# A first mixture of experts that adds its last four units by matrix multiplication instead of gathers

## The reference

```python
def moe_ffn(h, router_w, router_b, w_gate, w_up, w_down):
    ...
    w = jnp.take_along_axis(s, ids, axis=1)
    w = w / jnp.sum(w, axis=-1, keepdims=True)
    combine = jnp.sum(jax.nn.one_hot(ids, N_EXPERTS, dtype=jnp.float32) * w[..., None], axis=1)
    y = jnp.zeros(h.shape, jnp.float32)
    for e in range(N_EXPERTS):
        a = jax.nn.silu(h @ w_gate[e]) * (h @ w_up[e])
        y = y + combine[:, e:e + 1] * (a @ w_down[e]).astype(jnp.float32)
    return y.astype(h.dtype)
...
        x_lat = x_lat + g2 * ff_lat.reshape(x_lat.shape)
    return rms_norm(x_lat, final_g)
```

## Time and profile before

| | |
|---|---|
| median of 3 runs | 2612.09 us |
| profiled execution | 2609.95 us, span 2608.1 us |
| TensorE matmul busy | 2150.4 us (82%) |
| VectorE busy | 1245.8 us (48%) |
| ScalarE busy | 775.8 us (30%) |
| GpSimd busy | 203.5 us (8%) |
| DMA | 684.69 MB, mean 263 GB/s |

### The profile page before, as it was taken

How to read it: one execution, slowest core, us unless ns; L and a number is a source line. 1 busy time by engine, 2 the same in 40 slices (tenths; PEclk the granted TensorE clock), 3 DMA queues, 4 the chain that set the end, 5 groups by cost and what they waited for, 6 DMA issues and landing times. The chain is left out here.

```text
span 2608.1 us, 43444 instructions
## 1 busy us (share of the span) xinstructions
PE 2150.4 (82%) x18242; PEld 1499.7 (58%) x18242; DVE 1245.8 (48%) x1976; ACT 775.8 (30%) x1304; POOL 203.5 (8%) x202
## 2 busy tenths in 40 slices
PE   4999999896974999887778766899998887768765
PEld 3977777794542789543334335677777644334333
DVE  3367676645223544543333336666555653233334
ACT  4266666432113323211111114444423411111112
POOL 2010000101101000000000001111111000000001
PEclk8999999997997999898889887999999999889978
DMA  9157675438998233899999982211113699999995
GB/s 355 47 187 242 224 243 195 130 98 351 407 421 293 86 98 121 343 399 417 419 418 419 416 354 83 65 50 50 45 48 138 247 388 417 418 417 418 412 410 212
DMA packets 211850, 684.69 MB, mean 263 GB/s; under 512 B 23021, under 2 KB 122038, under 8 KB 152502
## 3 DMA queue, kind: packets, MB, share of 16 engines
q1 hardware_dynamic: 198742, 646.01, 64.4%
q0 software_dynamic: 8912, 21.04, 2.3%
q10 hardware_dynamic: 3984, 14.68, 1.4%
HBM read 671.68 MB, written 21.00 MB: 266 GB/s over the span
## 5 line engine op out<-in xcount | busy, mean ns | idle before, releaser
L221 PE MATMUL PS<-second 128*128 128x256 f32 (+1 forms) x4944 | 930.9, 346 | 54.2 <-DVE second L251 21.0
L221 PEld LDWEIGHTS PS<-second 128*128 128x128 f32 x4944 | 761.3, 193 | 200.3 <-DVE second L251 28.3
L221 PE MATMUL PS<-ring,arena 128*32 128x256 f32 (+5 forms) x6288 | 662.7, 453 | 208.9 <-DMA ring<-in_moe_w_down 65.6
L221 PEld LDWEIGHTS PS<-ring,arena 128*32 128x32 f32 (+2 forms) x6288 | 311.3, 124 | 449.6 <-issue 308.9
L221 PE MATMUL PS<-arena 128*32 128x256 f32 (+10 forms) x2480 | 496.1, 383 | 77.1 <-DMA ring<-in_moe_w_up 21.3
L221 PEld LDWEIGHTS PS<-arena 128*32 128x32 f32 (+4 forms) x2480 | 245.9, 151 | 241.2 <-issue 170.9
L233 ACT ACTIVATE arena<-PS 128x256 f32<-128x256 f32 (+2 forms) x218 | 106.5, 488 | 583.2 <-PE PS L221 506.0
L240 DVE TENSOR_TENSOR arena<-PS,arena 128x512 f32<-128x512 f32 (+1 forms) x305 | 210.5, 690 | 91.6 <-PE PS L221 64.7
L233 ACT ACTIVATE arena<-arena 128x128 f32<-128x128 f32 (+4 forms) x299 | 176.0, 589 | 191.8 <-DVE arena L240 67.3
L240 DVE TENSOR_TENSOR second<-ring,second 128x1024 fp32r<-128x1024 f32 (+1 forms) x90 | 149.0, 1656 | 156.1 <-ACT second L233 150.7
L240 DVE TENSOR_TENSOR arena<-arena,PS 128x256 f32<-128x256 f32 (+1 forms) x77 | 40.9, 531 | 372.3 <-PE PS L221 371.2
(11 more groups left out here) (170 smaller groups left out, 1358.3 us busy)
## 6 DMA issues: line engine op xcount, KB each, us to landing
ring<-in_moe_w_down SPq DMA_DIRECT2D x124, 1024.0 KB, 16.3
ring<-in_moe_w_up SPq DMA_DIRECT2D x121, 1024.0 KB, 15.4
ring<-in_moe_w_gate SPq DMA_DIRECT2D x109, 1024.0 KB, 16.6
ring<-in_ada_w SPq DMA_DIRECT2D x48, 1024.0 KB, 5.3
arena<-in_moe_w_gate SPq DMA_DIRECT2D x28, 1024.0 KB, 12.8
ring<-in_w_mod SPq DMA_DIRECT2D x22, 1024.0 KB, 7.0
arena<-in_moe_w_up SPq DMA_DIRECT2D x19, 1024.0 KB, 14.4
spare<-in_moe_w_gate SPq DMA_DIRECT2D x17, 1024.0 KB, 15.7
```

What stands on the lines that cost most here:

```text
L221: return P.e.matmul(o, l, r, start=st, stop=sp)
```

## The change

- Rows of units 8 to 11 no longer go to `y_d`. VectorE multiplies them with `GROW`, ScalarE and VectorE split the weighted rows into two fp32r parts (`down_ve`, `down_ac`), VectorE makes the 0/1 matrix (`where_late_ve`), and TensorE adds them to the tokens: unit 8 in iteration 10, unit 9 in iteration 11, units 10 and 11 together after the branch of the conditional units (`combine_late_pe`). VectorE adds the sums to `x` (`late_ve`).
- Two `shared` conditions fall, so the places and shares of these rows are computed early in the first mixture (`shares_pe`, `shares_ve`, `share_ve`, `columns_ve`).
- The eight gathers read only rows of units 0 to 7 and are issued once the gate matmuls of unit 11 are done. Their buffers move to the place of `XN` and `H2T` and are zero-filled by GpSimd, two in each of iterations 5 to 8.
- VectorE mixes tile 0 before it evicts unit 11 and tile 1 after it, both ahead of the branch. The order of the end is written out, and the last scaling to `XN` goes from ScalarE to VectorE.
- The router weights of the second mixture are loaded behind the second load of the convolution.

```diff
--- before.py
+++ after.py
@@ -1293,6 +1293,18 @@
+    LATE = 8
+    LATE_ROWS = [YP, *([second[AR0 + o][:, 2048 + 1024 * i:3072 + 1024 * i] for i in range(2)] for o in (12288, 27136))]
+    LATE_WT = [second[AR0 + 27136][:, 1024:1536], second[AR0 + 27136][:, 1536:2048], second[AR0 + 30976][:, 256:768]]
+    def late(n):
+        return (n + 1) % 2 if n < LATE + 4 else 2
+    def before_late(m, n):
+        return at("ps", "cm", m.i, n - 2 if n < LATE + 4 else n - 1, 3, 1) if n > LATE + 4 or LATE + 1 < n < LATE + 4 else None
@@ -1444,11 +1456,10 @@
-            else:
-                self.tokf, self.ws = tmp(NB, 4), tmp(NB)
+            self.tokf, self.ws = tmp(NB, 4), tmp(NB)
             self.tz, self.idx = tmp(NB), tmp(NB).bitcast(i32)
             self.ei, self.eii, self.nvi = tmp(NOV), tmp(NOV).bitcast(i32), tmp(1).bitcast(i32)
-            self.ybuf = [view(o + 1024 * j, F) for o, k in ((16384, 4), (14336, 2), (29768, 2)) for j in range(k)]
+            self.ybuf = [view(o + 1024 * t, F) for t in range(4) for o in (4096, 8192)]
@@ -1620,8 +1631,8 @@
-        if m.i < 2:
-            router_sp(MO[m.i + 1])
+        if m.i == 1:
+            router_sp(MO[2])
@@ -1688,6 +1699,37 @@
+    def late_pe(b, n, t, f, first, last):
+        W, rows_ = LATE_WT[late(n)], LATE_ROWS[late(n)]
+        for j in range(2):
+            i = mm(b, W[:, 128 * t:128 * t + 128], rows_[j][:, 512 * f:512 * f + 512], first and j == 0, last and j == 1)
+        return i
+    def combine_extra_pe(m, n):
+        P.wait_ge(at("W", m.i, n), at("ev", "down", m.i, n, 1))
+        for t in range(4):
+            for f in range(2):
+                late_pe(take(state["units"], "cm", m.i, n, t, f), n, t, f, True, True).then_inc(*P.mark("ps", "cm", m.i, n, t, f))
+    def combine_late_pe(m):
+        a, z = LATE + 2, LATE + 3
+        P.wait_ge(at("W", m.i, z), at("ev", "down", m.i, a, 1))
+        b4 = {}
+        for t in range(2):
+            for f in range(2):
+                b4[t, f] = take(state["units"], "cm", m.i, z, t, f)
+                late_pe(b4[t, f], a, t, f, True, False)
+        P.wait_ge(at("ev", "down", m.i, z, 1))
+        for t in range(4):
+            for f in range(2):
+                if t > 1:
+                    b4[t, f] = take(state["units"], "cm", m.i, z, t, f)
+                    late_pe(b4[t, f], a, t, f, True, False)
+                late_pe(b4[t, f], z, t, f, False, True).then_inc(*P.mark("ps", "cm", m.i, z, t, f))
@@ -1760,7 +1802,7 @@
-        b = take(state["units"], name, m.i, done=({"tok": "idx", "tok2": "idx2"}[name] if m.i == 0 else {"tok": "tokf", "tok2": "tokf2"}[name], m.i))
+        b = take(state["units"], name, m.i, done=("tokf2" if name == "tok2" else "tokf" if m.i else "idx", m.i))
@@ -1845,6 +1887,8 @@
+                if n > LATE + 1:
+                    combine_extra_pe(m, n - 2)
@@ -1855,8 +1899,7 @@
-                if m.shared:
-                    shares_pe(m, "share2", m.NV)
+                shares_pe(m, "share2", m.NV)
@@ -1871,10 +1914,14 @@
+            if m.shared is None:
+                combine_extra_pe(m, n)
...
+        else:
+            combine_late_pe(m)
@@ -1900,6 +1947,18 @@
+        if n >= LATE:
+            hi, lo = LATE_ROWS[late(n)]
+            V.wait_ge(at("ps", "frow", 1))
+            for f in range(2):
+                c = slice(512 * f, 512 * f + 512)
+                V.wait_ge(at("ps", "down" if f else "down0", m.i, n))
+                tt(DIAG[:, c], bank("down", m.i, n, f), GROW[:, c], ALU.mult, "gy", m.i, n, f)
+            for f in range(2):
+                c = slice(512 * f, 512 * f + 512)
+                V.wait_ge(at("hi", "y", m.i, n, f))
+                stt(lo[:, c], DIAG[:, c], m.ws[:, n:n + 1], hi[:, c].bitcast(f32), ALU.mult, ALU.subtract, "ev", "down", m.i, n, f)
+            return
@@ -1910,6 +1969,25 @@
+    def where_late_ve(m, n):
+        V.wait_ge(before_late(m, n))
+        tt(LATE_WT[late(n)].rearrange("p (t s) -> p t s", s=128), bc(iota[:, :].unsqueeze(1), 4, 128), bc(m.tokf[:, n, :].unsqueeze(2), 4, 128), ALU.is_equal, "W", m.i, n)
+    def late_ve(m, n, t):
+        for f in range(2):
+            o = x[:, t, 512 * f:512 * f + 512]
+            V.wait_ge(at("ps", "cm", m.i, n, t, f))
+            tt(o, bank("cm", m.i, n, t, f), o, ALU.add, "ev", "cm", m.i, n, t, f)
+    def mix_ve(m, t):
+        V.wait_ge(at("comb", m.i, 2 * t))
+        stt(m.ybuf[2 * t], m.ybuf[2 * t], m.w12[:, t, 0:1], x[:, t, :], ALU.mult, ALU.add)
+        V.wait_ge(at("comb", m.i, 2 * t + 1))
+        stt(x[:, t, :], m.ybuf[2 * t + 1], m.w12[:, t, 1:2], m.ybuf[2 * t], ALU.mult, ALU.add)
@@ -2124,20 +2202,17 @@
-                shares_ve(m, "share2", m.NV)
+            shares_ve(m, "share2", m.NV)
...
-                share_ve(m, "share2", m.NS, m.NB)
+            share_ve(m, "share2", m.NS, m.NB)
...
-                columns_ve(m, m.NS, m.NB)
+            columns_ve(m, m.NS, m.NB)
@@ -2159,6 +2234,8 @@
+            if m.shared is None and n in (LATE - 2, LATE - 1):
+                where_late_ve(m, n + 2)
@@ -2171,6 +2248,10 @@
+                if n > LATE + 1:
+                    for t in range(4):
+                        late_ve(m, n - 2, t)
+                    where_late_ve(m, n)
@@ -2183,7 +2264,11 @@
         count = count_of(m, V)
+        if m.shared is None:
+            mix_ve(m, 0)
         down_ve(m, m.NP - 1)
+        if m.shared is None:
+            mix_ve(m, 1)
 
@@ -2193,6 +2278,10 @@
+            if m.shared is None:
+                where_late_ve(m, n)
+                for t in range(4):
+                    late_ve(m, n, t)
@@ -2220,18 +2309,25 @@
-        def mix(t):
-            V.wait_ge(at("comb", m.i, 2 * t))
-            stt(XN[:, t, :], m.ybuf[2 * t], m.w12[:, t, 0:1], x[:, t, :], ALU.mult, ALU.add)
-            V.wait_ge(at("comb", m.i, 2 * t + 1))
-            stt(x[:, t, :], m.ybuf[2 * t + 1], m.w12[:, t, 1:2], XN[:, t, :], ALU.mult, ALU.add, "mix", m.i, t)
         def final(t):
             V.wait_ge(at("sq", "m0", t))
             stt(x[:, t, :], x[:, t, :], rs[:, t:t + 1], FROW, ALU.mult, ALU.mult, "x", "m0", t)
 
-        V.wait_ge(at("ev", ("row", m.i), 1), at("ev", "frow", 1))
-        tiles_ve(mix, final)
+        V.wait_ge(at("ev", "frow", 1))
+        late_ve(m, LATE + 3, 0)
+        late_ve(m, LATE + 3, 1)
+        final(0)
+        mix_ve(m, 2)
+        late_ve(m, LATE + 3, 2)
+        final(1)
+        mix_ve(m, 3)
+        late_ve(m, LATE + 3, 3)
+        norm_x_ve("m0", 0)
+        final(2)
+        norm_x_ve("m0", 1)
+        final(3)
+        norm_x_ve("m0", 2)
+        norm_x_ve("m0", 3)
@@ -2250,6 +2346,14 @@
+        if n >= LATE:
+            hi = LATE_ROWS[late(n)][0]
+            A.wait_ge(at("ev", "share2", m.i), *((at("y", m.i, LATE - 2), at("y", m.i, LATE - 1)) if n == LATE + 1 else ()), before_late(m, n))
+            for f in range(2):
+                c = slice(512 * f, 512 * f + 512)
+                A.wait_ge(at("gy", m.i, n, f))
+                act(hi[:, c], DIAG[:, c], ACT.Copy, "hi", "y", m.i, n, f, scale=m.ws[:, n:n + 1])
@@ -2315,15 +2419,19 @@
-        overflow(m, A, count, one, D("y0"), D("y1"))
+        overflow(m, A, count, one)
...
-            A.wait_ge(at("ev", "cm", m.i, m.NB - 1, t, 1) if m.shared else at("mix", m.i, t))
+            A.wait_ge(at("ev", "cm", m.i, m.NB - 1 if m.shared else LATE + 3, t, 1))
...
-            tiles_ac(name, first, lambda t: again_ac(name, t))
+            first(0)
+            for t in range(4):
+                if t < 3:
+                    first(t + 1)
+                again_ac(name, t)
@@ -2357,6 +2465,16 @@
+            if 5 <= n <= 8 and m.i == 0:
+                G.wait_ge(at("xn_d", m.i), at("ps", "down", m.i, 0), at("ps", "gu", m.i, 2, 0))
+                for o in m.ybuf[2 * n - 10:2 * n - 8]:
+                    fill(o, 0.0, "yz")
+        if m.shared is None:
+            G.wait_ge(at("yi", m.i), at("y", m.i, LATE - 2), at("y", m.i, LATE - 1), at("yz"), at("ps", "gu", m.i, LATE + 3, 0))
+            for i in range(8):
+                G.e.indirect_dma_start(
+                    out=m.ybuf[i], out_offset=None, in_=m.y_d, in_offset=bass.IndirectOffsetOnAxis(ap=m.yi[:, i // 2, i % 2:i % 2 + 1], axis=0),
+                    bounds_check=LATE * m.R - 1, oob_is_err=False).then_inc(*state["comb"][i].next("comb", m.i, i))
         count = count_of(m, G)
         overflow(m, G, count, lambda n: gather_gp(m, n))
@@ -2364,13 +2482,6 @@
-            return
-        G.wait_ge(at("yi", m.i), at("y", m.i, m.NB - 2), at("y", m.i, m.NB - 1))
...
-                out=m.ybuf[i], out_offset=None, in_=m.y_d, in_offset=bass.IndirectOffsetOnAxis(ap=m.yi[:, i // 2, i % 2:i % 2 + 1], axis=0),
-                bounds_check=m.NY - 1, oob_is_err=False).then_inc(*state["comb"][i].next("comb", m.i, i))
@@ -2398,6 +2509,8 @@
+            if n == 1:
+                router_sp(MO[1])
```

(8 more changed lines are left out.)

## The result

The changed kernel takes 2619.99 us (median of 6 runs, 2618.43 to 2625.07), the kernel before 2611.25 beside it (6 runs): a ratio of 1.0031, 95% interval 1.0021 to 1.0041, so 8 to 9 us slower. Measured a second time (8 runs) the ratio was 1.003 (1.002 to 1.004). The prediction was 2613.1 with a range of 2605 to 2618, so the measured time lies above the range. The profiled execution took 2618.57 us, span 2616.6.

A forecast was written before the change was run, and what follows sets the result against it. Weights, then VectorE, bound the first mixture's end. Removed waiting (10.2 us) and scalings (2.4) against early delay, VectorE/ScalarE work, low-clock TensorE and tail additions gave +1.0: profiled 2611.0, median 2613.1, range 2605 to 2618.

The forecast's parts named there:

- a shift of the goal is a shift of the time: After the convolution's first VectorE scaling: everything keeps its order, so a shift there shifts the whole time equally.
- Early shares, +2.0: Iteration 1: 8 more f32 matmuls on TensorE delay the weights, and the delay passes through; +2.0 us, bounds 0 and 2.5.
- Up of unit 10: Weight-bound part: up matmuls of unit 10 start at 782.3, from 781.23 + 2.0 early − 0.9 for a write.
- Down of unit 9 waits for the third addition: Its first bank is freed by VectorE's third addition for unit 8 at 791.2, so down ends at 794.9.
- Additions of unit 9 in 6.3 us: VectorE's eight additions for unit 9: first sum at 804.4, additions to 810.7, 0/1 matrix done at 811.4.
- D: Rival, chance 0.15: late-landing gathers hold VectorE at the mix of tile 0, ahead of unit 11's eviction; +6.5, 2619.6 us.
- The branch: VectorE's skip holds TensorE's sums for unit 10 until 823.1, after the mix of tile 1; jump free, bounds 0 and 2.1.
- B: Rival, chance 0.10: the skip doesn't hold TensorE, so additions follow the mix of tile 1 at once; −4.65, 2608.4 us.
- C: Rival, chance 0.20: the skip doesn't hold TensorE and the early 2.0 hides too, or units 9 to 11 shorten equally; 2606.4.
- Evictions and restart: End of the mixture: 3.0 us per late unit's eviction; after the branch eight low-clock matmuls (3.36) and 1.23 to first addition.
- The split beside GpSimd: Before the convolution's own chain: ScalarE makes one half of its weights in 1.91 us, VectorE the other in 2.29.
- predicted goal: Start of the convolution's own chain, its first VectorE scaling: 853.1 against 852.06 before.

The follow-up runs named there:

- x8: Kernel before plus the early shares alone, their eight matmuls and copy in unit 4 instead of unit 1: ratio 1.0002.
- x9: Changed kernel whole, with the eight matmuls of the early shares and their copy in unit 4 instead of unit 1: ratio 1.0020.
- x1: Changed kernel with the second mixture's router loads back in their old place, before the branch: ratio 1.0038.
- x3: Changed kernel with the sums of token tile 0 in the two side PSUM banks that no conditional unit takes: ratio 1.0010.
- x4: Changed kernel with the eight gathers issued after unit 11's down matmuls instead of after its gate matmuls: ratio 1.0044.
- x5: Changed kernel with only units 10 and 11 added by TensorE; units 8 and 9 written out and gathered like the first eight: ratio 1.0011.
- x6: Changed kernel with only units 10 and 11 added by TensorE, first tile's sums in side banks, tile 2 mixed before tile 1's additions: ratio 0.9996.
- x7: Changed kernel, only units 10 and 11 by TensorE, first tile's sums in side banks, tile 2 mixed before tile 1's additions, shares in unit 4: ratio 0.9981.

## Why the prediction was wrong

Of the predicted +1.0 us and the measured +8 to +9, the mixture's part has +5.0 (mean of two executions each: 235.7 against 230.7), the convolution +2.4. The rest, 0.6 to 1.6, I can't place. Two steps failed: the time of the additions of unit 9 and what follows them in front of the branch, and the sentence that a shift of the goal is a shift of the time.

- **Early shares, +2.0: right where they stand.** The next group of TensorE (two transposes, at 658.66 before) started at 658.47 after, so +1.74 by the first gather. Up of unit 10 at 161.34 us from the gather against 160.27: +1.07, predicted +1.1.
- **"What follows hangs on it and keeps its order, so a shift of the goal is a shift of the time": the step that failed most in kind.** The order was kept to 0.4 us for some 190 us, and then the stretch at the lower clock lasted 10.3 us instead of 6.9, which is 1.6 of the convolution's 2.4 us. x8 and x9, with eight matmuls moved from unit 1 (390 us ahead of this stretch) to unit 4, had the short stretch, but so had x1 and x3 with these matmuls in their place. A sum of instruction durations taken from one profile doesn't see this.
- **Down of unit 9 waits for the third addition.** `down_pe` takes both its banks first, so it waited for the fourth (790.14, right behind the addition of 789.35): a term 0.8 us too small.
- **Additions of unit 9 in 6.3 us: the largest single miss of the mixture's part.** They took 8.0, with two stops beside the gathers, and x4 without gathers there took 6.26. I had a rival in which gathers hold VectorE (D, 0.15), but by landing late; they landed in time. That its 2619.6 lies beside the measured 2620.0 is luck, since its mechanism didn't occur. In sum, the 0/1 matrix of unit 11 ended 192.9 us after the first gather, 190.4 predicted.
- **The branch: right.** TensorE started on VectorE's L58 and nothing else, 10.92 us idle. B and C were wrong. The jump over 76 operations was free (0.20 from the end of the mix to TensorE's start), as taken. By the Trainium skill's page Runtime: NRT & Kernel Launch (Instruction fetch mechanics) it should have been, and the rows agree.
- **Evictions and restart.** The evictions took 3.2 instead of 3.0 twice, with 0.24 for a hand-over, so that from the 0/1 matrix to the end of the mix of tile 1 it was 12.3 us instead of 11.5. The first addition came 3.97 us after the restart instead of 4.6: the granted clock was 0.50 in 824 to 826 and 1.00 again from 828, where I had the lower level for all eight matmuls. From the first late addition to the last square chain 20.92 us, predicted 20.95.
- **The split beside GpSimd.** The convolution's low half took 2.79 us instead of 2.29, because it now starts while GpSimd's row operation (850.19, 1.89) still runs: +0.5, a collision made by an engine that became earlier. The Trainium skill's page SBUF — State Buffer (SBUF: two separate sides) has this case (two SBUF inputs against a GpSimd operation that reads SBUF), and here row and rule agree.

Together in the first profile: 0.8 + 1.7 + 0.8 − 0.6 + 0.5 = 3.2 us, by which the mixture's part missed 232.1. The predicted goal was itself +1.0, so the change's design had no reserve: 10.2 us of waiting were removed and as much work put in their place, most of it on VectorE, which then sets the end.

## What to carry to other kernels

Move to another engine only as many of the last pieces as the wait to be hidden needs: of four units by matmul, the last two alone made the mixture's part 0.8 to 1.6 us shorter than before (x5), and with a better hand-over 5 to 6 (x6, x7); with the other two it was 5 us longer. Look for hand-overs that pass through a branch by the bank rotation: spare banks removed a 4.2 us wait, of which 1.5 came back. Put added matmuls where the engine waits for data in the trace, not where their inputs first exist; here the ratio was 0.0010 to 0.0018 lower in each of three pairs of kernels, though the intervals of each pair overlap. Before a stage that does the same work is called slower by the change, compare how long TensorE stood at the lower clock in it, in more than one profile.

## What the runs showed of the hardware

- Additions from PSUM on VectorE stopped for 0.45 and 1.46 us beside the last two of eight indirect gathers issued by GpSimd (1.30 us apart); without gathers there, 6.26 us for eight instead of 7.96. In the five profiles with gathers beside them the eight took 8.0 to 8.7. The first four additions, beside earlier gathers, did not stop; in the second profile of that kernel it was the first five.
- A VectorE operation of 128x2048 with two SBUF inputs took 2.79 us when it started beside a GpSimd tensor operation, 2.29 when it started behind it.
- After an idle time of 2.1 us TensorE's granted clock fell to 0.50 for 6.9 us (eight profiles) or 10.3 us (six), though TensorE was busy throughout and did the same work. It was 10.3 where the clock fell at most 0.5 us after TensorE's restart, and 6.9 where it fell 1.2 to 2.4 us after it.
